# Two transformer blocks, fp32 in three fp32r products: quadrant products accumulate in PSUM on copies that ScalarE writes, and one double's products interleave with the next's

## Reference

```python
h = h + 0.5 * swiglu_ffn(rmsnorm(h, g1), w_in, w_out)     # first FFN
h = h + mixer_1(rmsnorm(h, g))
h = h + 0.5 * swiglu_ffn(rmsnorm(h, g2), w_in, w_out)     # second FFN
h = rmsnorm(h, norm_final)                                # end of block one
h = h + 0.5 * swiglu_ffn_2(rmsnorm_2(h, g3), w_in, w_out) # third FFN
h = h + mixer_2(rmsnorm_2(h, g))
h = h + 0.5 * swiglu_ffn_2(rmsnorm_2(h, g4), w_in, w_out) # fourth FFN
# swiglu: gate, up = split(x @ w_in); (silu(gate) * up) @ w_out
```

## Time and profile before

| | |
|---|---|
| time, median of 3 runs | 2157.51 us (2157.3 to 2158.07) |
| the profiled execution | 2157.14 us, span 2155.3 us |
| mean granted TensorE clock | 0.998 |
| busy: PE / PEld / DVE / ACT / POOL | 2140.4 / 1899.4 / 1561.7 / 891.9 / 166.0 us |

### The profile page before, as it was taken

One profiled execution on the slowest core, in us unless ns is written; L12 is line 12 of the kernel. 1 busy time (PEld: TensorE's weight loads), 2 busy tenths in 40 slices (PEclk: granted clock), 3 DMA queues, 4 the chain that ended last, 5 costly groups with the idle time before them and its releaser, 6 DMA issues.

```text
span 2155.3 us, 30597 instructions
## 1 busy us (share of the span) xinstructions
PE 2140.4 (99%) x12718; PEld 1899.4 (88%) x12718; DVE 1561.7 (72%) x1798; ACT 891.9 (41%) x1110; POOL 166.0 (8%) x135
## 2 busy tenths in 40 slices
PE   9999999999999999999999999999999999999998
PEld 7998998888777888998998898998788888998997
DVE  8975976453466548984898897697788768874983
ACT  6532533242233425541445543344572356442443
POOL 0000003610123100000000000000102002000002
PEclk9999999999999999999999999999999999999999
DMA  4332332232222223332242233233222123332231
GB/s 162 108 128 69 108 118 98 98 118 95 81 79 78 80 88 116 108 128 78 99 134 84 79 106 127 79 99 108 88 69 69 50 86 111 99 127 79 98 132 45
DMA packets 59176, 210.39 MB, mean 98 GB/s; under 512 B 6560, under 2 KB 8992, under 8 KB 58784
## 3 DMA queue, kind: packets, MB, share of 16 engines
q1 hardware_dynamic: 58464, 205.30, 28.3%
q0 software_dynamic: 288, 2.62, 0.3%
q10 hardware_dynamic: 288, 0.52, 0.1%
HBM read 206.33 MB, written 2.10 MB: 97 GB/s over the span
## 4 chain that ended last, share of the span: by engine, by line
PE 94%; DVE 4%; ACT 1%; issue 1%; DMA 0%; SPq 0%; DVEq 0%; ACTq 0%
PE accs L672 25%; PE accs L673 25%; PE accs L674 25%; PE mixbs L674 3%; PE mixbs L673 3%; PE mixbs L672 3%; PE mixbs L1240 1%; PE mixbs L1217 1%; DVE w_lo L1834 1%; PE accs L1179 1%; PE accs L1178 1%; PE accs L1177 1%; ACT w_hi L1301 0%; PE mixbs L1059 0%; DVE rstd L1969 0%
## 5 line engine op out<-in xcount | busy, mean ns | idle before, releaser
L1301 ACT ACTIVATE w_hi<-w_raw 128x1024 fp32r<-128x1024 f32 x497 | 515.4, 1054 | 600.6 <-PE accs L674 281.9
L1834 DVE TENSOR_TENSOR w_lo<-w_raw,w_hi 128x1024 fp32r<-128x1024 f32 x497 | 613.7, 1238 | 108.9 <-ACT w_hi L1301 102.6
L672 PE MATMUL accs<-x_hi,w_hi 128*128 128x512 f32 (+1 forms) x1408 | 490.7, 349 | 2.1 <-DVE x_lo L1901 1.8
L674 PE MATMUL accs<-x_hi,w_lo 128*128 128x512 f32 (+1 forms) x1408 | 484.0, 344 | 0.0
L673 PE MATMUL accs<-x_lo,w_hi 128*128 128x512 f32 (+1 forms) x1408 | 483.8, 344 | 0.0
L672 PEld LDWEIGHTS accs<-x_hi,w_hi 128*128 128x128 f32 x1408 | 267.0, 190 | 35.6 <-DVE x_lo L1901 3.1
L674 PEld LDWEIGHTS accs<-x_hi,w_lo 128*128 128x128 f32 x1408 | 266.9, 190 | 32.0
L673 PEld LDWEIGHTS accs<-x_lo,w_hi 128*128 128x128 f32 x1408 | 267.2, 190 | 29.9
L672 PE MATMUL accs<-hid_hi,w_hi 128*128 128x512 f32 (+1 forms) x714 | 275.8, 386 | 0.0
L673 PE MATMUL accs<-hid_lo,w_hi 128*128 128x512 f32 (+1 forms) x714 | 275.7, 386 | 0.0
L674 PE MATMUL accs<-hid_hi,w_lo 128*128 128x512 f32 (+1 forms) x714 | 275.6, 386 | 0.0
(11 more groups left out here) (408 smaller groups left out, 3086.5 us busy)
## 6 DMA issues: line engine op xcount, KB each, us to landing
w_raw<-weights SPq DMA_DIRECT2D x383, 512.0 KB, 3.2
y_t<-h SPq DMA_DIRECT2D x16, 128.0 KB, 1.9
h<-x_t SPq DMA_DIRECT2D x3, 512.0 KB, 6.4
k1c<-const POOLq DMA_DIRECT2D x1, 1536.0 KB, 7.7
k2c<-const POOLq DMA_DIRECT2D x1, 1024.0 KB, 7.7
h<-x_t ACTq DMA_DIRECT2D x2, 256.0 KB, 4.0
w_raw<-weights SPq DMA_DIRECT2D x1, 384.0 KB, 4.8
cst<-const SPq DMA_DIRECT2D x1, 161.0 KB, 7.8
```

The source lines that it names most:

```text
L672: pe.matmul(bank, w_hi[:, n % HI_SLOTS, w], hi, start=start, stop=False, skip_group_check=read_between)
L674: return pe.matmul(bank, w_lo[LO[n]][:, w], hi, start=False, stop=stop, skip_group_check=read_between)
L1301: act.activation(w_hi[:, n % HI_SLOTS, :], w_raw[RAW[n]][:, :], ACT.Copy).then_inc(hi_split, 1)
L1834: dve.tensor_tensor(w_lo[LO[n]][:, :], w_raw[RAW[n]][:, :], w_hi[:, n % HI_SLOTS, :].bitcast(F32), ALU.subtract).then_inc(lo_split, 1)
```

## The change

The line-numbered functions of before are above. The change does four things.

1. **Banks accumulate.** ACT writes -P1 from `r_a` into `r_b` ("neg"); P6 then accumulates on it in PSUM, and P7 on top. P7's result, P6 - P1, is copied to `f_s` by ACT between ("snap"), P5 in `r_c` is copied to `f_up` ("five"), and P3 and P4 accumulate in `r_c` and `r_b`. ACT copies the last up quadrant (`f_up`, "c21"). Per double DVE has four combining passes in place of seven, ACT five acts beside the splits in place of two (hidden rounding aside).
2. **Order.** The products stand as P1 P5 P6 P2 P7 P3 P4, and P1 of the next double comes before P3 and P4 of this one. After the last double of a pass, unit 0 of the output stage takes that place. `weight_sum` order becomes s3, s1, s2, s4.
3. **Output sequence of pass 1.** `_begun = 3`: three tiles (m = 0, 1, 2) run over their early parts first, then all three get their last two, so tiles 0 and 1 end at the 26th and 28th part in place of the 18th and 20th; tile 2 and the later ones end where they did.
4. **Where doubles begin.** In `plain_only`, `plain_first` and `plain_next` the same calls now prepare P5 as the second unit (it needs s1), and s2, which P6 needs, is made in that call or, in the third FFN, behind it.

The diff, cut (the DVE loop over doubles, where the seven passes stood, now calls `up_late`, the pass at `r_a`, and `gate_late` between `prepare` calls):

```diff
-PRODUCTS = ("p1", "p6", "p2", "p7", "p5", "p4", "p3")
-P1, P6, P2, P7, P5, P4, P3 = range(7)
+
+
+PRODUCTS = ("p1", "p5", "p6", "p2", "p7", "p3", "p4")
+P1, P5, P6, P2, P7, P3, P4 = range(7)
...
 UNIT0 = {d: n0 for d, n0, plain in ALL}
 SEVEN = {d: i for i, d in enumerate(d for d, n0, plain in ALL if not plain)}
-DOUBLE_AT = {UNIT0[d] + i: (d, i) for d in SEVEN for i in range(7)}
+UNITS = {}
+for _f in range(4):
+    for _p in range(2):
+        _seven = [x for x in doubles(_f, _p) if not x[2]]
+        for _i, (_d, _n, _plain) in enumerate(_seven):
+            UNITS[_d] = [_n + (_j + 1 if _j > P7 else _j - (2 if _i and _j == P1 else 0)) for _j in range(7)]
+DOUBLE_AT = {n: (d, i) for d in UNITS for i, n in enumerate(UNITS[d])}
+
+
+def out_unit(f, p, u):
+
+    return FIRST[f"ffn{f}_out{p}"] + (u if u else -2)
+
...
     _early = _nk - 2
-    _seq = [(m, k) for m in range(2) for k in range(_early)] + [(m, k) for m in range(2) for k in range(_early, _nk)]
-    _seq += [(m, k) for m in range(2, 8) for k in range(_nk)]
+    _begun = 3 if _p else 2
+    _seq = [(m, k) for m in range(_begun) for k in range(_early)]
+    _seq += [(m, k) for m in range(_begun) for k in range(_early, _nk)]
...
+            def quadrant(d, i, bank, first_of=None):
+
...
+            def first_product(d, drain):
+
+                pe.wait_ge(*((drained, drain - 2) if drain else (quad, made(d - 1, "c11"))))
+                quadrant(d, P1, r_a)
+
+            def last_products(d):
+
+                pe.wait_ge(quad, made(d, "c22"))
+                quadrant(d, P3, r_c)
+                quadrant(d, P4, r_b)
+
+            def middle_products(f, d):
+
+                if SEVEN[d]:
+                    pe.wait_ge(quad, made(seven_before(d), "c12"))
+                quadrant(d, P5, r_c, first_of=f if d % sum(HALVES) == NPLAIN[f] else None)
+                pe.wait_ge(f_acted, acted(d, "neg"))
+                quadrant(d, P6, r_b)
+                quadrant(d, P2, r_a)
+                pe.wait_ge(f_acted, acted(d, "snap"))
+                quadrant(d, P7, r_b)
 
...
+                            first_product(d, drain)
+                            if i and d - 1 in SEVEN:
+                                last_products(d - 1)
+                            middle_products(f, d)
                         drain = drain + 4 if plain else 0
-                    out_tiles(f, p)
+                    out_tiles(f, p, range(1))
+                    last_products(d)
+                    out_tiles(f, p, range(1, 2 * HALVES[p]))
 
...
+            def quadrants_end(d):
+
+                act.wait_ge(quad, made(d, "gate"))
+                act.activation(f_gate[:, :, :], f_gate[:, :, :], ACT.Silu).then_inc(f_acted, 1)
+                act.wait_ge(block_done, UNITS[d][P4] + 1)
+                act.activation(f_up[:, :, t1], r_b, ACT.Copy).then_inc(f_acted, 1)
...
-                        split(n0 + P7)
+                        at, begins = UNITS[d], d - 1 not in SEVEN or i == 0
+                        if begins:
+                            split(at[P1] + 2)
+                        split(at[P1] + 3)
+                        if not begins:
+                            split(at[P1] + 4)
+                            split(at[P1] + 5)
+                            quadrants_end(d - 1)
+                        act.wait_ge(block_done, at[P1] + 1)
+                        if begins:
+                            act.wait_ge(drained, OUT0[f"ffn{f}_in{p}"] + 4 * i)
+                        else:
+                            act.wait_ge(f_acted, acted(d - 1, "c21"))
+                        act.activation(r_b, r_a, ACT.Copy, scale=-1.0).then_inc(f_acted, 1)
+                        split(at[P5] + 3)
+                        split(at[P6] + 3)
                         if i:
                             round_hidden(d - 1)
-                        split(n0 + P5)
-                        split(n0 + P4)
-                        split(n0 + P3)
-                        split(n0 + 7)
-                        split(n0 + 8)
-                        split(n0 + 9)
-                        act.wait_ge(quad, made(d, "gate"))
-                        act.activation(f_gate[:, :, :], f_gate[:, :, :], ACT.Silu).then_inc(f_acted, 1)
+                        act.wait_ge(block_done, at[P6] + 1)
+                        if SEVEN[d]:
+                            act.wait_ge(quad, made(seven_before(d), "c12"))
+                        act.activation(f_s[:, :, :], r_b, ACT.Copy).then_inc(f_acted, 1)
+                        split(at[P2] + 3)
+                        if not begins:
+                            act.wait_ge(hid_done, HID_COUNT[d - 1] - 1)
+                        act.activation(f_up[:, :, t2], r_c, ACT.Copy).then_inc(f_acted, 1)
+                        split(at[P7] + 3)
+                    split(out_unit(f, p, 0) + 3)
+                    split(out_unit(f, p, 0) + 4)
+                    quadrants_end(d)
                     first = FIRST[f"ffn{f}_out{p}"]
                     for u in range(2 * HALVES[p]):
+                        if u == 1:
+                            round_hidden(d)
                         if u:
                             split(first + u + LEAD)
-                        else:
-                            round_hidden(d)
                         if p:
                             for m in range(KD):
                                 if OUT_END[p][m] // 8 == u:
...
             def before(n):
 
-                if n + 1 in DOUBLE_AT and DOUBLE_AT[n + 1][1] == P1:
-                    weight_sum(DOUBLE_AT[n + 1][0], "s3")
-                if n in DOUBLE_AT:
-                    d, i = DOUBLE_AT[n]
-                    if i in (P1, P2, P7):
-                        weight_sum(d, {P1: "s2", P2: "s4", P7: "s1"}[i])
+                if n in DOUBLE_AT and DOUBLE_AT[n][1] == P1:
+                    weight_sum(DOUBLE_AT[n][0], "s3")
+                if n + 1 in DOUBLE_AT and DOUBLE_AT[n + 1][1] == P5:
+                    weight_sum(DOUBLE_AT[n + 1][0], "s1")
+                if n in DOUBLE_AT and DOUBLE_AT[n][1] == P5:
+                    weight_sum(DOUBLE_AT[n][0], "s2")
+                if n in DOUBLE_AT and DOUBLE_AT[n][1] == P2:
+                    weight_sum(DOUBLE_AT[n][0], "s4")
 
             def prepare(n):
...
                     chained_mean()
                 prepare(n0 + 3)
                 if f == 2:
+                    weight_sum(d + 1, "s3")
                     chained_sum()
-                before(n0 + 4)
-                if f != 2:
-                    split(n0 + 4)
+                if f == 2:
+                    weight_sum(d + 1, "s1")
+                else:
+                    prepare(n0 + 4)
                 invert_root("norm3b" if f == 2 else f"norm{r}", rstd[:, :])
                 gate_plain(d, n0, a, 0)
...
-                prepare(n0 + 5)
+                if f == 2:
+                    split(n0 + 5)
                 up_plain(d, n0 + 3, a, 1)
+                if f == 2:
+                    before(n0 + 5)
+                else:
+                    prepare(n0 + 5)
+
+            def up_late(d):
+
+                dve.wait_ge(block_done, UNITS[d][P7] + 1)
+                dve.wait_ge(f_acted, acted(d, "five"))
+                dve.tensor_tensor(f_up[:, :, t2], r_b, f_up[:, :, t2], ALU.subtract).then_inc(quad, 1)
+
+            def gate_late(d):
+
+                dve.wait_ge(block_done, UNITS[d][P3] + 1)
+                dve.wait_ge(f_acted, acted(d, "snap"))
+                dve.tensor_tensor(f_gate[:, :, t2], r_c, f_s[:, :, :], ALU.subtract).then_inc(quad, 1)
+                dve.wait_ge(quad, made(d, "c12"))
+                dve.tensor_tensor(f_gate[:, :, t2], f_gate[:, :, t2],
+                                  rstd[:, :].unsqueeze(1).to_broadcast([P, 2, S])[:, :, t2], ALU.mult).then_inc(quad, 1)
 
             def ffn(f):
                 after = [1, 3, 4, 6][f]
```

More of the change, by code:

```diff
@@ L624, in made, with acted, seven_before @@
         def made(d, name):
[L626 to L630 removed]
+            return 4 * SEVEN[d] + ["c11", "c22", "c12", "gate"].index(name) + 1
+        def acted(d, name):
+            before = sum(2 if plain else 5 for e, n0, plain in ALL[:d])
+            return before + (["neg", "snap", "five", "silu", "c21"].index(name) if d in SEVEN else name) + 1
+        def seven_before(d):
+            return max(e for e in SEVEN if e < d)
         def hid_of(d):
```

161 lines of the change are left out of this document (64 added, 97 removed).

## The result

The changed kernel takes 2164.4 us (median of 8 runs, 2163.7 to 2164.7) and the kernel before 2157.6 (median of 8, 2157.1 to 2158.1). The ratio is 1.0031, with a 95% interval of 1.0021 to 1.0041: slower by 6.8 us, where 5.9 were forecast. The profiled execution has a span of 2162.8 us; it was 2155.3.

A forecast was written before the change was run, and what follows sets the result against it. PE, busy 99% of the span, was taken to bound the kernel. Doubles 0, output stage 4.3 and doubles' starts 1.6 sum to 5.9 us on the 2157.5 median: 2163.4 us, range 2159.0 to 2167.5.

The forecast's parts named there:

- the doubles: 0: In all 38 steady seven-product doubles PE never waits, with 1.4 us to spare at r_b: 0 us.
- The output stage, +4.3: Second FFN's last output stage: tile 0 ends eight parts later, tile 2 starts 4.3 us late, none regained: +4.3 us.
- Full, with ACT's hand-overs: Second FFN's last output stage: DVE, busy 44.66 of 54.50 us, was said to have no slack between tiles.
- Where the doubles begin, +1.6: Starts of the seven-product doubles: late s1 and s2 cost 0.7 (third FFN), 0.6 (first), 0.3 us (second).
- The sum, 5.9: Whole kernel: 4.3 + 0.7 + 0.6 + 0.3 = 5.9 us slower, giving 2163.4 us.
- A: Second FFN's tiles 0 to 7: DVE absorbs the 4.3 us delay; all regained gives 2159.1 us; 20%.
- D: Whole kernel: freed DVE time removes stalls before doubles and the norm's wait, delay absorbed too: 2155.5 us; 3%.
- B: Steady doubles: ACT late at r_b makes every double wait; 0.1 us each gives 2167.2 us; 8%.
- C: After the new 2.4 us gap PE's clock falls, one spell of 4.3 us: 2167.7 us; 3%.

The follow-up runs named there:

- the tiles alone: The kernel before with three tiles begun ahead in the second output stages, nothing else: 2162.0 us, ratio 1.0023.
- the experiment that went by the first reading: The changed kernel with the norm3 sums (a copy and seven additions) moved from DVE to GpSimd, three tiles kept: 2167.8 us, ratio 1.0048.
- s3's move: The changed kernel with two tiles, earlier s2, x_hi ahead of the square, and s3 one unit earlier in the first FFN: 2155.9 us, ratio 0.9992.

## Why the prediction was right

**What bounds the kernel; the doubles: 0.** Right. There is no wait in the steady doubles, `r_b` has 1.4 us of slack, as worked out, and one rounding more on ACT used 1.0 of it free of charge.

**The output stage, +4.3.** Measured 4.1 in the trace, 4.6 with the tiles alone, 4.2 when they are taken out. The chain of late starts came as written: tile 2 4.3 late, stops of 0.7 and 0.3 at units 6 and 7, 2.4 at x_lo, the rest at the norm's sum. The reason was stated too simply. "Full, with ACT's hand-overs" read DVE's 44.66 busy of 54.50 us as the limit; from tile 2 on the limit is the loop of hand-overs. The delay is the same in both readings, since neither leaves slack, so the number could not tell them apart. But what follows for a remedy differs, and the experiment that went by the first reading lost 3.4 us.

**Where the doubles begin, +1.6.** Measured, beyond the stops of before: third FFN 0.8 (0.7 forecast), second 0.45 (0.3), first 0.8 (0.6), 2.1 in all. The causes named hold for the third and second: P5 starts 0.6 early (a stop of 0.81 for 1.41), P6 waits for neg behind s2, and the edit that moves s2 and one rounding took the stops away. For the first the forecast had one stop, at `xm_lo`. The trace has two, at the low part of P5 (57.25, which goes with s3's move) and at `xm_lo` (59.11, which stays), so the size is right there for a reason that is only half the forecast's.

**The sum, 5.9.** By place the trace has 4.1 + 2.1 = 6.2; the medians differ by 6.8. In the profiled executions the first norm sum, at 22.5 us, is already 0.6 later in the changed kernel, and the tail behind the last matmul 0.5 longer, and with these the span's 7.5 is nearly whole. The first norm sum varies from 22.5 to 24.2 us among the profiles here, also of kernels that begin alike (22.97 with the tiles alone, which starts as the kernel before does), so I don't count it to the change; what the remaining 0.6 between the medians is stays open.

**The rivals.** A (the delay is absorbed) and D (faster) did not come: there was no slack, for the reason just given. B did not either. C, a clock that falls after the new stop, did not come in the changed kernel's profile but did in other executions, for 0.2 to 0.8 us and not the 4.3 it was priced at; it is told below.

## What to carry to other kernels

- When two engines pass tiles to each other, ask which instructions are on the loop between them, not how busy each is. A write that the other engine waits for goes ahead of one that it does not; that was worth 1.5 and 2.0 us here, while cutting 3.7 us of busy time that was not on the loop gave 0.45.
- An order that gives one stage more cover (a third tile begun ahead) takes it from whoever consumes the first result. Check every stage that shares the order: in one of four it cost 4.2 us. Begun two tiles ahead, and with the hidden low part made first, that stage had no need of the third.
- Freeing an engine's time on average (69 us of DVE) is worth nothing unless it was waited for; the late places are at the seams, where one phase's order meets the next.
